# Seven half-size products for eight: Strassen's scheme for the first 3,072 units of a feed-forward down projection

## The reference

```python
x = layer_norm(DN_ALPHA * x + cross_attn(x, mem_k, mem_v, xq_w, xo_w), ln2_g, ln2_b)
f = jnp.square(jax.nn.relu(x @ w1 + b1)) @ w2 + b2        # w1: 1024 x 4096, w2: 4096 x 1024
x = layer_norm(DN_ALPHA * x + f, ln3_g, ln3_b)
```

## Time and profile before

| | us |
|---|---|
| median of 3 runs | 1415.48 |
| the profiled execution | 1416.35 |
| its span, first instruction to last | 1414.5 |
| PE busy | 1362.3 |
| weight loads (beside PE) | 1315.7 |
| DVE busy | 716.1 |
| POOL busy | 659.0 |
| ACT busy | 362.8 |

### The profile page before, as it was taken

One profiled execution on the slowest core, in us unless ns is written; L12 is line 12 of the kernel. 1 busy time (PEld: TensorE's weight loads), 2 busy tenths in 40 slices (PEclk: granted clock), 3 DMA queues, 4 the chain that ended last, 5 costly groups with the idle time before them and its releaser, 6 DMA issues.

```text
span 1414.5 us, 20772 instructions
## 1 busy us (share of the span) xinstructions
PE 1362.3 (96%) x8472; PEld 1315.7 (93%) x8472; DVE 716.1 (51%) x852; ACT 362.8 (26%) x696; POOL 659.0 (47%) x431
## 2 busy tenths in 40 slices
PE   6999989998899999989999999999999999999995
PEld 6999978797899978989999999999999999999995
DVE  5899994356513753496762125521155311455366
ACT  4222432334512431154320012200022100222223
POOL 3476987344832724549333333333333333335412
PEclk9999999999999999999999999999999999999998
DMA  8223432110011375101111111111111111112112
GB/s 253 65 49 79 121 125 75 30 45 16 30 45 31 112 261 194 60 0 50 41 44 45 44 45 47 47 51 49 45 46 44 45 45 44 45 45 60 45 45 79
DMA packets 44417, 93.55 MB, mean 66 GB/s; under 512 B 20288, under 2 KB 26688, under 8 KB 41920
## 3 DMA queue, kind: packets, MB, share of 16 engines
q1 hardware_dynamic: 34592, 89.73, 20.4%
q10 hardware_dynamic: 9760, 2.93, 0.8%
HBM read 85.39 MB, written 7.25 MB: 65 GB/s over the span
## 4 chain that ended last, share of the span: by engine, by line
PE 74%; DVE 16%; POOL 3%; issue 2%; ACT 2%; DMA 1%; SPq 0%; DVEq 0%; ACTq 0%; POOLq 0%
PE bank L668 23%; PE bank L669 23%; PE bank L670 22%; DVE conv_sum L1682 11%; POOL x_low L568 1%; ACT x_full L1432 1%; DVE bank L1809 1%; ACT x_high L1436 1%; POOL w_low L368 1%; DMA x_full<-xT_in 1%; PE conv_sum L985 1%; PE bank L960 1%; PE conv_sum L819 1%; PE conv_sum L668 0%; PE conv_sum L670 0%
## 5 line engine op out<-in xcount | busy, mean ns | idle before, releaser
L668 PE MATMUL bank<-x_high,w_high 128*128 128x384 f32 (+1 forms) x1200 | 390.6, 326 | 13.7 <-POOL w_low L368 11.4
L669 PE MATMUL bank<-x_low,w_high 128*128 128x384 f32 (+1 forms) x1200 | 387.9, 323 | 0.0
L670 PE MATMUL bank<-x_high,w_low 128*128 128x384 f32 (+1 forms) x1200 | 387.4, 323 | 0.0
L366 POOL TENSOR_TENSOR w_high<-w_raw,ones 128x1024 fp32r<-128x1024 f32 x75 | 143.4, 1912 | 441.2 <-issue 222.2
L668 PE MATMUL bank<-mix,w_high 128*128 128x384 f32 (+1 forms) x832 | 272.9, 328 | 3.4 <-issue 1.9
L669 PE MATMUL bank<-mix,w_high 128*128 128x384 f32 (+1 forms) x832 | 273.3, 328 | 0.0
L670 PE MATMUL bank<-mix,w_low 128*128 128x384 f32 (+1 forms) x832 | 270.9, 326 | 0.0
L668 PEld LDWEIGHTS bank<-x_high,w_high 128*128 128x128 f32 x1200 | 225.8, 188 | 15.0 <-POOL w_low L368 10.2
L669 PEld LDWEIGHTS bank<-x_low,w_high 128*128 128x128 f32 x1200 | 225.9, 188 | 0.1
L670 PEld LDWEIGHTS bank<-x_high,w_low 128*128 128x128 f32 x1200 | 225.8, 188 | 0.0
L368 POOL TENSOR_TENSOR w_low<-w_raw,w_high 128x1024 fp32r<-128x1024 f32 x75 | 183.7, 2450 | 5.9
(11 more groups left out here) (287 smaller groups left out, 1965.7 us busy)
## 6 DMA issues: line engine op xcount, KB each, us to landing
w_raw<-slabs_in SPq DMA_DIRECT2D x110, 512.0 KB, 3.6
dec_kv<-dec_kv_in SPq DMA_DIRECT2D x16, 1024.0 KB, 5.4
scratch<-slabs_in SPq DMA_DIRECT2D x8, 512.0 KB, 3.6
yT_res<-ffn_sum SPq DMA_DIRECT2D x4, 768.0 KB, 3.5
x_full<-xT_in SPq DMA_DIRECT2D x4, 384.0 KB, 5.3
x_full<-xT_in SPq DMA_DIRECT2D x2, 768.0 KB, 9.2
x_full<-xT_in SPq DMA_DIRECT2D x2, 576.0 KB, 11.2
yT_res<-ffn_sum SPq DMA_DIRECT2D x4, 288.0 KB, 2.6
```

Source lines behind the costliest of these rows:

```text
L366: pool.tensor_tensor(high[:, slot, :], raw[:, p, :], one, ALU.mult).then_inc(high_done, 1)
L668: pe.matmul(out, w_high, x_high, start=first, stop=False)
L669: pe.matmul(out, w_high, x_low, start=False, stop=False)
L670: return pe.matmul(out, w_low, x_high, start=False, stop=last)
```

## The change

Down products of the first 3,072 hidden units (three of the four down stages, 24 slabs) go by Strassen's scheme (Winograd's form). The product [out features] x [hidden units] x [tokens] is halved in all three directions: two halves of 512 output features, 2 blocks of 128 hidden units each, two halves of 528 tokens (`HT`). Eight block products become seven, made of sums of the blocks. One group is 512 hidden units (`GROUPS` = 6), its four units (`UNITS`) are the four pairs of output blocks; a unit has seven products, a product has 2 banks x 2 blocks x 3 = 12 matmuls of 264 columns. So there are 24 units of 84 matmuls where 24 slabs of 72 stood.

What it needs beside the matmuls:
- All 32 up slabs come first (stage W1, one block by block). ACT makes the relu and DVE the square; the square goes to DRAM (`hidden_out`), not into `q`.
- For each group SP fetches four forms of the hidden units from DRAM (`forms_in`), DVE makes four more by sums (`form_sums`, 1,056 numbers per partition each, of two SBUF tensors); 7 of them enter the products, ACT makes 7 high parts (`form_high`), DVE 3 low parts and POOL 4 (`form_low`). There are two sets of forms, one in `q`, one where `x` was. Group G+1 is made ready in the units of group G.
- For each unit DVE makes four sums of weight quarters (`unit_weight_sums`, 256 numbers each, one buffer); ACT makes a high part and POOL a low part of each of the seven weight forms (`w_form_high`, `w_form_low`), in eight slots.
- After each product DVE takes two banks (528 numbers) and adds them to one of three sums or to `acc` (`add_product`; the first time for three of them a copy). PE may be four products ahead. In the last group 7 more additions per unit bring the sums together (`join`).
- The last 1,024 hidden units are fetched back to `q` in the last group, cut by ACT (`hidden_high`), POOL and DVE (`hidden_low`), and go through the same last down stage as before. Its first two slabs are cut by POOL after the last unit's forms.

The eight banks are one tensor now, and some semaphores are shared; that changes names, not instructions.

```diff
+UP = FF // P
+S_ST = S_FF + UP
+GROUPS, UNITS = 6, 4
+NU = GROUPS * UNITS
+HT = T // 2
+FORM_HIGHS = (0, 5, 6, 2, 3, 1, 4)
+BY_DVE_FORMS, BY_POOL_FORMS = (2, 3, 1), (0, 5, 6, 4)
...
# SP
+        def forms_in(G):
...
+            else:
+                sp.wait_ge(sem("st_done"), 7 * UNITS * (G - 1))
+            k = 4 * G
+            for i, lo, t in ((6, k + 2, HT), (3, k, HT), (0, k, 0), (5, k + 2, 0)):
+                sp.dma_start(forms_full[b][:, i], hidden[:, lo:lo + 2, t:t + HT]).then_inc(sem("forms_in"), 16)
...
+        for U in range(NU):
+            sp.wait_ge(sem("w_form_low"), 7 * U + 6)
+            sp.wait_ge(sem("weight_sums"), 4 * (U + 1))
+            load(S_ST + U + 2, U % 2)
+            if U % UNITS == 0 and U // UNITS + 1 < GROUPS:
+                forms_in(U // UNITS + 1)
+            if U == NU - UNITS:
+                sp.wait_ge(sem("st_done"), 7 * (NU - UNITS))
+                for j in range(NB - 1):
+                    last_hidden_in(j)
# POOL
+        for U in range(NU):
+            G = U // UNITS
+            for i in range(7):
+                w_form_low(U, i)
...
+                if U >= NU - 3 and i in (2, 5):
+                    hidden_low(2 * (U - NU + 3) + i // 5)
+        hidden_low(6)
+        pool.wait_ge(sem("st_done"), 7 * NU - 4)
+        split(LATE, 0, LAST // 2, MEM_SLABS, freed=S_ST)
# PE
+        def unit_product(U, i):
+
+            G, f, b = U // UNITS, 7 * U + i, U // UNITS % 2
+            if U % UNITS == 0:
+                pe.wait_ge(*form_order(i, G))
+            pe.wait_ge(sem("w_form_low"), f + 1)
...
+                pe.wait_ge(sem("st_added"), f - 3)
+            for c in range(2):
+                out = ps[2 * k + c][:, 0:HT // 2]
+                t = slice(c * HT // 2, (c + 1) * HT // 2)
+                for kb in range(2):
+                    w = slice(kb * P, (kb + 1) * P)
+                    last = product(out, wh_forms[:, f % 8, w], wl_forms[:, f % 8, w], forms_high[b][:, i, kb, t],
+                                   forms_low[b][:, i, kb, t], kb == 0, kb == 1)
# ACT
+        def w_form_high(U, i):
...
+                act.wait_ge(sem("st_done"), f - 7)
...
+            act.copy(wh_forms[:, f % 8, :], weight_source(U, i)).then_inc(sem("w_form_high"), 1)
+
+        def hidden_high(*blocks):
+
+            for j in blocks:
+                act.wait_ge(sem("forms_in"), 64 * GROUPS + (112 if j < 7 else 128))
+                act.copy(q[:, j, 0, :], qf[:, j, T:BLK]).then_inc(sem("form_high"), 1)
...
+                if U >= NU - 3 and i in (1, 4):
+                    hidden_high(2 * (U - NU + 3) + i // 4)
# DVE
+        def unit_weight_sums(U):
+
+            b11, b12, b21, b22 = (raw[:, U % 2, k * 256:(k + 1) * 256] for k in range(4))
+            t1, t2, t3, t4 = (weight_sums[:, k, :] for k in range(4))
+            dve.wait_ge(*unit_raw(U))
+            if U:
+                dve.wait_ge(sem("w_form_low"), 7 * U)
...
+            tt(t1, b12, b11, ALU.subtract).then_inc(sem("weight_sums"), 1)
+            tt(t3, b22, b12, ALU.subtract).then_inc(sem("weight_sums"), 1)
...
+        for p in range(2):
+            dve.wait_ge(sem(f"hidden_out{p}"), 16 * UP // 2)
+        unit_weight_sums(0)
+        for U in range(NU):
+            G, r = divmod(U, UNITS)
+            for i in range(7):
+                add_product(U, i)
+                if i == 0 and U + 1 < NU:
+                    unit_weight_sums(U + 1)
+                if G + 1 < GROUPS:
+                    if (r, i) in ((1, 2), (1, 4), (2, 1), (2, 3)):
+                        form_sums(G + 1, {(1, 2): 2, (1, 4): 3, (2, 1): 1, (2, 3): 4}[r, i])
+                    if r == 3 and i in (0, 2, 4):
+                        form_low(G + 1, BY_DVE_FORMS[i // 2])
+                elif i >= 2:
+                    join(r, i)
```

364 lines of the change are left out of this document (260 added, 104 removed).

## The result

The changed kernel takes 1455.89 us (median of 4 runs, 1454.89 to 1457.46) against 1415.01 for the kernel before in the same comparison: ratio 1.029, 95% interval 1.0277 to 1.0304. The forecast was 1444 us, slower. The profiled execution took 1456.86 us; its span is 1455.1, 40.6 more than before.

What follows compares the result with a forecast made beforehand. PE bounds the kernel before; in the new units DVE, waiting for POOL, would set the pace. 7.6 + 230 + 61.5 + 7.7 = 306.8 us against 278.4, +28.4, gave about 1444 us; forecast 1430 to 1460, range 1409 to 1465.

Steps and rivals of the forecast that it cites:

- PE, and DVE without waits: Per group of four units: 264-column matmuls 0.1225 us apart, PE 41.2 us; DVE's own work 36.7 us.
- DVE against POOL: In every unit, DVE's two-SBUF-input instructions wait 0.34 us for POOL; 23 waits add 7.8, so DVE needs 44.5 us a group.
- The new wait: At the change of groups, DVE's single weight-sum buffer waits for POOL's late low parts: 1.5 us, making a group 46.0.
- The start: Before the first products: PE idle 5.9 us for first weight forms and sums, 1.7 lost to the clock; 7.6 us.
- The last group: PE waits for seven transfers, then POOL's queue ends the group: 61.5 us, bounds 47 and 69.
- The end: After the last unit: PE idle 6 us while POOL cuts the first late slab, 1.7 for the clock; 7.7 us.
- Parts at nothing: Up slabs keep 11.6 us; ACT's casts, POOL's early long parts, DRAM traffic and removed up-stage parts change nothing.
- PE's pace in five groups: Rival: collisions fall in DVE's slack, five groups take 206 us instead of 230; 1420 us, chance 0.18.
- all hidden: Rival: only hand-overs show, PE's pace and last group at its lower bound; 1407 us, faster, chance 0.14.

Runs made afterwards that it cites:

- spread: Changed kernel with the preparation of the next group's forms spread over the group's four units, single buffer of weight sums kept; 1447.2 us.
- short_dve_lows: Changed kernel with DVE's three long low parts of each group from the second on cut to 8 of 528 columns; 1443.1 us.
- moved_only: Changed kernel with POOL's four long low parts of each group from the second on moved to DVE, nothing else; 1439.2 us.
- dve_lows: spread2_last2 with all seven long low parts of groups 2 to 6 on DVE, forms fetched at each group's start, first weight sums formed earlier; 1396.3 us.
- spread2_last2: Changed kernel with two weight-sum buffers, form work spread, POOL's long low parts halved, last group's hidden units fetched earlier, cuts and joins partly put off; 1426.4 us.
- last_moved: Changed kernel with the last group's seven transfers of hidden units issued 7 us earlier, their casts and low parts one unit later; 1449.6 us.
- short_pool_lows: Changed kernel with POOL's four long low parts of each group from the second on cut to 8 of 528 columns; 1423.0 us.

## Why the prediction was right, and where not

The sign, the range (1430 to 1460) and the order of the terms held; the time was 12 us too low. PE's pace stands. The number for the middle groups (46.0 forecast, 47.05 measured) came out near by a wrong path, and that is luck.

**PE, and DVE without waits.** 0.1225 forecast, 0.122 measured: right. An addition lasts 0.697 as forecast, but the next one starts 0.62 after it (1111.46 and 1112.08 above) and not 0.73: over 28 of them DVE needs 3.1 us less than the 36.7 forecast.

**DVE against POOL.** The step that failed in its mechanism. Forecast: DVE needs 44.5 us a group and sets the pace, since a DVE instruction with two SBUF inputs comes "at a random moment" and waits 0.34, in every unit. The text set its own tests: wrong if DVE waits for PE in most units, or if the weight sums take their 0.42. DVE waits for PE in each of the four units, 4.2 us in a group together, and two of the four weight sums take their 0.42. DVE is busy only 38.0 us in the mean of the middle groups, its waits for the ports included; these add up to 5.5 where 7.8 were forecast, and in slack units they cost nothing. POOL's own waits, some 5.1 us a group on its short low parts, are as large; the forecast counted them only in passing.

What binds is the hand-over. By the rows of DVE and POOL, from 1101.3 to 1124.7 one of POOL's instructions or one of DVE's with two SBUF inputs is always in progress: 23.4 us without a gap, from the start of the last unit to the fifth product of the next first one. PE's idle times of the group (3.14 and 1.22) fall in them or begin there. In the rest of the group there are gaps, 4.35 us in all. The same count for five kernels, as the mean of four groups, each from its second unit's weight sums to the next group's:

| kernel | sum | group, us | one of them in progress | neither |
|---|---|---|---|---|
| changed kernel | 47.0 | 47.28 | 42.93 | 4.35 |
| spread | 47.0 | 45.67 | 43.10 | 2.57 |
| short_dve_lows | 43.1 | 44.35 | 39.99 | 4.36 |
| moved_only | 42.2 | 44.66 | 37.82 | 6.84 |
| dve_lows | 42.2 | 40.98 | 37.11 | 3.86 |

So the forecast's own numbers (30.7 + 16.3 = 47.0) would have given the group's 47.05, but that the two agree is in part chance: the ports are not taken all the time, and some own work runs beside the other engine's (a blocked instruction gets 0.15 to 0.3 us of itself done). The sum says which work to cut, not how long a group lasts: spread took 45.3 for 47.0, and for 42.2 the groups took 44.7 and 41.0. That both sides count is shown: the group fell by 6.2 us with POOL's long low parts cut, by 2.7 with DVE's cut, by 2.4 with four moved. That they exclude each other for whole instructions rests on rows such as 2.60 above, not on a run that measured it alone. The Trainium skill (SBUF — State Buffer, section Who interferes with whom) calls it an exclusive lock for the whole instruction, whichever side starts first. The trace agrees on both sides, but for those 0.15 to 0.3 us: 2.60 for DVE's 0.42, 1.75 for POOL's 0.74.

**The new wait.** Forecast 1.5 us a group, 46.0 in all; measured: five groups 235.5 without the start's stall, 5.5 above the 230. The wait stands as seen (36.8 us in 12 waits), but removing it brought 1.25 us a group. Missing in the sum was the half clock behind each hand-over: fourth group 0.96, about 1.7 us.

**The start.** 7.6 forecast, about 5.4 measured: idle 1.9, 3.2 and 0.3, with the wait for the square in DRAM as described. The 1.7 us at half clock did not come: the granted clock is 1.00 from 1018 to 1038. In dve_lows, which forms the first sums before that wait, the second of these idle times falls from 2.95 to 0.68 us, and the first group takes 42.0 us from its first matmul, against 50.5 here and 44.8 in spread2_last2 with the old start. (The early sums were not tried alone.)

**The last group.** 61.5 forecast with 69 as upper bound; 71.1 measured, the largest miss, outside its bounds. Its first part came out right by two errors that cancel. The transfers were issued from 1264.04 on, 5.4 us after the group's start, since SP takes the slab's turn first, where the forecast had them at its start; and they landed by 1276.5, 12.5 us after the first issue, where 17 were forecast. PE goes on 20.1 us after the group's start, against 19.5. The miss lies behind that: 50.9 us to the group's end, where 42.0 (40.5 and 1.5) stood. The forecast let POOL's queue end the group. POOL's last weight form was done at 1317.27, 38.5 us on, but PE then had five products to do instead of one, and they took 12.2 us. DVE's queue held it back: DVE is busy 42.5 of the 50.9 us, and PE waits 3.93, 3.80 and 3.78 us for additions. The first of these waits comes behind one of DVE for POOL's last short low part (10.29 us once) that was in no term. Nor was the clock, 0.81 in this group: PE's 41.0 us of work took 52.3 us. How much of that would show in the time without the waits, no run says.

```profile
1278.73:1320.98 42.25, 30.08 (x180) 28.95 (x181) 34.02 (x35) 10.91 (x22) 34.31 (x26) 0.78 0.12 38
1320.98:1329.65 8.67, 8.66 (x49) 8.51 (x50) 8.50 (x11) 0.00 (x0) 4.26 (x2) 0.66 0.02 3
```

last_moved shows 8.2 us of the group as the place of the transfers and casts; the rest is DVE's and POOL's work, as the fall to 50.0 with fewer joins and shorter low parts shows (those two were not tried apart).

**The end.** 7.7 forecast, 6.8 measured, by another cause than the one named. The split of the first late slab was in time. The last hidden block, which the forecast called hidden, was not: its transfer waits for DVE's joins, went out at 1328.63, and its low part lasted 3.39 us beside POOL's cutting of a late slab.

**Parts at nothing.** Held: 11.62 us per up slab, +0.6 in all.

**Rivals.** "PE's pace in five groups" (1420) was right that the collisions fall in DVE's slack, and "all hidden" (faster) that the transfers are fast; both left out the hand-over. short_pool_lows (1423) and dve_lows (1396) come near the two, once the hand-over is cleared.

## What to carry to other kernels

Where POOL and DVE both read SBUF tensors, add up POOL's time and the time of DVE's instructions with two SBUF inputs, and compare the sum, not each engine's share, with PE's time, above all for the stretch in which both fall due. While the sum stood at 47 against PE's 41, order, buffers and halves gained at most 1.8 us a group; at 42.2 the same means gained 3.7. A long elementwise step then belongs on the engine that does it faster (1.3 us on DVE against 2.5 on POOL), even if that engine looks fuller. When an edit shortens one wait exactly as computed and the total stays, look one stage later for the same microseconds before trying the next order. And a term that comes out right is no proof of its path: here one engine's forecast waits and a group's length agreed with the measurement while the engine named was idle for 9 us of 47.
